# Dense FFN and output projections: 512 and 128 tokens in place of twice 320 per weight block

## The reference, cut to what matters

```python
def trunk_layer(x, cond, l, p, ctx, rope):
    ...
    mix, new_ctx = token_mixer(modulate(x, p['norm_mix'][l], sh_m, sc_m), p, l, ctx, rope)   # ends in mixed @ w_out[l]
    x = x + g_m * mix
    h = modulate(x, p['norm_ffn'][l], sh_f, sc_f)
    f = swiglu(h, ffn_w_gu, ffn_w_down)          # layer 0
    return x + g_f * f

def swiglu(h, w_gu, w_down):
    g, u = jnp.split(h @ w_gu, 2, axis=-1)
    return (jax.nn.silu(g) * u) @ w_down
```

## Time and profile before

| | |
|---|---|
| median of 3 runs | 2766.9 us (2763.91 to 2770.16) |
| profiled execution, its own time | 2763.11 us |
| its span, first to last instruction | 2761.4 us |
| TensorE matmuls / weight loads busy | 2425.1 us / 2202.9 us |
| VectorE, ScalarE busy | 1454.2 us, 1068.7 us |
| TensorE's mean granted clock | 0.93 |

### The profile page before, as it was taken

One profiled execution on the slowest core, in us unless ns is written; L12 is line 12 of the kernel. 1 busy time (PEld: TensorE's weight loads), 2 busy tenths in 40 slices (PEclk: granted clock), 3 DMA queues, 4 the chain that ended last, 5 costly groups with the idle time before them and its releaser, 6 DMA issues. The chain is left out here.

```text
span 2761.4 us, 47069 instructions
## 1 busy us (share of the span) xinstructions
PE 2425.1 (88%) x19300; PEld 2202.9 (80%) x19300; DVE 1454.2 (53%) x2061; ACT 1068.7 (39%) x1753; POOL 319.4 (12%) x340
## 2 busy tenths in 40 slices
PE   6995778988899999989967788886999999999993
PEld 4984555777899999989845657786899999999992
DVE  5576555675422222245765646753455555455556
ACT  4332235673422122142321456733444444354443
POOL 0055333000000000000642320002000000000002
PEclk8998897998999999999978969997999999999996
DMA  5333756502222322223136200024775676567654
GB/s 211 88 83 61 217 178 203 192 1 78 61 77 58 86 76 65 60 55 94 46 75 199 73 1 1 1 61 146 214 213 177 195 234 201 172 213 228 197 176 166
DMA packets 453116, 340.49 MB, mean 123 GB/s; under 512 B 90961, under 2 KB 421151, under 8 KB 451935
## 3 DMA queue, kind: packets, MB, share of 16 engines
q1 hardware_dynamic: 436383, 277.43, 34.6%
q10 hardware_dynamic: 11520, 41.95, 4.7%
q0 software_dynamic: 5056, 18.88, 1.8%
HBM read 287.68 MB, written 50.53 MB: 122 GB/s over the span
## 5 line engine op out<-in xcount | busy, mean ns | idle before, releaser
L2294 PE MATMUL ps<-h_hi,w_hi 128*128 128x256 f32 x1408 | 398.9, 283 | 2.1 <-DVE h_lo L2437 2.1
L2294 PE MATMUL ps<-h_hi,w_lo 128*128 128x256 f32 x1408 | 398.6, 283 | 0.0
L2294 PE MATMUL ps<-h_lo,w_hi 128*128 128x256 f32 x1408 | 398.5, 283 | 0.0
L2445 DVE TENSOR_TENSOR w_lo<-w_raw,w_hi 128x2048 fp32r<-128x2048 f32 (+1 forms) x180 | 309.1, 1756 | 118.9 <-ACT w_hi L2343 118.9
L2294 PEld LDWEIGHTS ps<-h_hi,w_hi 128*128 128x128 f32 x1408 | 270.0, 192 | 5.1 <-issue 2.3
L2294 PEld LDWEIGHTS ps<-h_lo,w_hi 128*128 128x128 f32 x1408 | 270.0, 192 | 2.8
L2294 PEld LDWEIGHTS ps<-h_hi,w_lo 128*128 128x128 f32 x1408 | 270.0, 192 | 0.0
L2343 ACT CAST w_hi<-w_raw 128x2048 fp32r<-128x2048 f32 (+1 forms) x180 | 256.4, 1473 | 0.1
L2678 PE MATMUL ps<-ffn_h_hi,w_hi_ffn 128*128 128x320 f32 x704 | 161.5, 311 | 5.5 <-DVE ffn_h_lo L378 4.2
L2678 PE MATMUL ps<-ffn_h_lo,w_hi_ffn 128*128 128x320 f32 x704 | 161.2, 310 | 0.0
L2678 PE MATMUL ps<-ffn_h_hi,w_lo_ffn 128*128 128x320 f32 x704 | 161.0, 310 | 0.0
(11 more groups left out here) (442 smaller groups left out, 5619.8 us busy)
## 6 DMA issues: line engine op xcount, KB each, us to landing
w_raw<-in_moe_w_gu SPq DMA_DIRECT2D x182, 512.0 KB, 5.1
w_raw<-in_moe_w_down SPq DMA_DIRECT2D x91, 512.0 KB, 5.9
G_decay<-in_ada_w ACTq DMA_DIRECT2D x54, 512.0 KB, 5.0
w_ahead<-in_ffn_w_gu SPq DMA_DIRECT2D x44, 512.0 KB, 5.2
slots_h<-tm SPq DMA_DIRECT2D x13, 1024.0 KB, 11.1
slots_y<-tm SPq DMA_DIRECT2D x12, 1024.0 KB, 11.2
w_ahead<-in_ffn_w_down SPq DMA_DIRECT2D x16, 704.0 KB, 4.7
oA<-in_ada_w ACTq DMA_DIRECT2D x20, 512.0 KB, 5.0
```

Source lines behind the costliest of these rows:

```text
L2294: mm = pe.matmul(ps[:, j % 2, half * BLK:(half + 1) * BLK], gu(wt, j, half, k), x[:, k, :], start=(k == 0 and n == 0), stop=(k == KC - 1 a ...
L2445: dve.tensor_tensor(wlo[:, q, part], raw[:, q, part], whi[:, q, part].bitcast(F32), ALU.subtract).then_inc(s["lo_d" if down else "lo_u"], 1)
```

## The change

A new constant WIDE, ((0, 512), (512, 640)), takes the place of HALVES, ((0, 320), (320, 640)), in the output projections and the dense FFN: the matmuls of each weight block now move 512 tokens and then 128, into the same two banks. ScalarE's Silu and VectorE's product go by the same pieces. In PIECES the cut between the banks moves too, so that `add_chunk` takes 0 to 128, 128 to 512 and 512 to 640. The norms and the input projection keep HALVES.

```diff
-PIECES = ((0, P, 0, 0), (P, T // 2, 0, 1), (T // 2, T, 1, 1))
+WIDE = ((0, 512), (512, T))
+PIECES = ((0, P, 0, 0), (P, 512, 0, 1), (512, T, 1, 1))
...
                             for n, (wt, x) in enumerate(((ws.hi, self.mhi), (ws.hi, self.mlo), (ws.lo, self.mhi))):
-                                for j, (a, b) in enumerate(HALVES):
+                                for j, (a, b) in enumerate(WIDE):
                                     mm = pe.matmul(ps[:, 2 * (m % 4) + j, 0:b - a], wt[:, m % 2, k * P:(k + 1) * P], x[:, k, a:b],
...
         for a, b, half, j in PIECES:
             x = self.xT[:, m, a:b]
-            a0 = HALVES[half][0]
+            a0 = WIDE[half][0]
...
                                     for m, (wt, x) in enumerate(((ws.hi, hhi), (ws.hi, hlo), (ws.lo, hhi))):
-                                        for st, (a, b) in enumerate(HALVES):
+                                        for st, (a, b) in enumerate(WIDE):
                                             mm = pe.matmul(ps[:, 4 * (j % 2) + 2 * half + st, 0:b - a], wt[:, u, o:o + P], x[:, k, a:b],
...
                                 for m, (wt, x) in enumerate(((ws.hi, ahi), (ws.hi, alo), (ws.lo, ahi))):
-                                    for st, (a, b) in enumerate(HALVES):
+                                    for st, (a, b) in enumerate(WIDE):
                                         mm = pe.matmul(ps[:, 2 * (m_ % 4) + st, 0:b - a], wt[:, u, j * P:(j + 1) * P], x[:, j, a:b],
...
-                            for st, (a, b) in enumerate(HALVES):
+                            for st, (a, b) in enumerate(WIDE):
                                 act.activation(sg[:, n % 2, a:b], ps[:, 4 * (n % 2) + st, 0:b - a], ACT.Silu).then_inc(s["silu"], 1)
...
-                            for st, (a, b) in enumerate(HALVES):
+                            for st, (a, b) in enumerate(WIDE):
                                 dve.wait_ge(s["silu"], 2 * c + st + 1)
                                 g = sg[:, n % 2, a:b]
                                 dve.tensor_tensor(g, g, ps[:, 4 * (n % 2) + 2 + st, 0:b - a], ALU.mult).then_inc(s["prod"], 1)
```

## The result

The changed kernel takes 2865.47 us (median of 4 runs, 2860.34 to 2869.57) against 2766.66 for the one before (4 runs): a ratio of 1.0362, 95% interval 1.035 to 1.0375. It is slower by 98.8 us; forecast were 91.6 us and 2858 us, with a range of 2838 to 2902. The profiled execution took 2860.3 us, with a span of 2858.6.

The account below looks back on a forecast made before the run. TensorE's matmul stream was taken to bound the kernel. Pairs 89.7, half clock 1.6 and bare chain 0.3 sum to 91.6 us, giving 2854.7 us on the profiled execution and 2858 on the median; range 2838 to 2902.

Parts of the forecast that it names:

- The load of the wide matmul: Edited matmul lines: its weight load has only the 128-wide matmul as cover, so pairs grow 45.6 ns, 89.7 us in all.
- The size, 112 ns for that step: Edited lines: a 128-wide matmul lasts as long as the next weight load, 112 ns, with bounds 104 to 122.
- The one-column rows: Trace of the kernel before: ten one-column matmuls whose weight loads come 115 and 111 ns apart, taken as the load's length.
- Half clock: First 6 to 10 us of matmul bursts: the half-speed loss grows with a pair's period, +1.6 us if it doubles.
- the bare chain: Where down matmuls wait for the last tile's Silu and product: unequal pieces add 0.15 us net, twice, 0.3 us.
- Rival A: Edited lines: the narrow matmul is cover enough for the load, a pair stays 293.1 ns, 2767 us; chance 0.07.
- The straight line through 320 and 512 columns: Matmul time from two measured widths: 0.418 ns a column plus 12.9 ns fixed, so 66.4 ns for 128 columns.
- formula for the gap: The Trainium skill's rule for back-to-back matmuls: columns / 2.4 plus 2.5 ns, a pair 271.7 ns before and after.
- Rival B: Edited lines: recorded narrow-matmul starts at face value, a 55 ns step, a pair 281.7 ns, gain 22 us, 2745 us; chance 0.03.
- the 12.9 ns fixed: Part of each matmul's time independent of its columns, from the 320- and 512-wide steps.
- Rival C: Edited lines: the whole 134 ns between loads is the price, 67.6 ns a pair, 133 us, 2902 us; chance 0.10.
- The signs given: Profile after: starts in turns of 0.23 and 0.11 us, pair 0.339, FFN 551 us, projections 67, longer ScalarE and VectorE waits.

Follow-up runs that it names:

- experiment 1: Changed kernel with 512-wide matmuls taking only 64 of 128 weight columns, 128-wide ones all: down pair 286.8 ns, total 2758.05 us.
- experiment 2: Changed kernel with 128-wide matmuls taking only 64 of 128 weight columns, 512-wide ones all: pairs 340.0 to 343.4 ns, total 2866.57 us.
- 3: Changed kernel with 512-wide matmuls taking 96 of 128 weight columns: down pair 313.4 ns, total 2822.16 us.
- 4: Changed kernel with the cut at 448 (448 and 192 tokens), all computed: 2813.22 us, +44.6 on the kernel before.
- experiment 5: Changed kernel with the cut at 384 (384 and 256 tokens), all computed: 2765.95 us against 2765.47 for the kernel before, ratio 1.0006.
- 9: Changed kernel with the 128-token piece of each weight block before the 512-token one, all computed: 2852.57 us beside 2762.5 for the kernel before.
- experiment 6: Changed kernel with the 512-wide matmuls left out of the three edited lines: 213 ns a step at granted clock 0.50, total 2608.9 us.
- experiment 11: Changed kernel run once more unaltered: 2871.49 us; up bursts 346.7 and 343.3 ns a pair, down bursts 340.0.
- experiment 10: Kernel cut at 448 with its 448-wide matmuls left out of the edited lines: 111 ns a step, granted clock 0.91, total 2449.34 us.
- experiment 8: Changed kernel with, from the second up tile on, all gate-block matmuls before all up-block ones: up line 345.0 ns a pair, total 2872.74 us.

## Why the prediction was right

**The load of the wide matmul is what the change uncovers: right, and shown.** Experiments 1 and 2 shorten one load each (and with it the output features of that matmul), with the same moving columns, 3 gives the slope, 4 and 5 the point where it begins (192 columns too few, 256 enough), 9 that identical weights don't help. The Trainium skill (TensorE: Matmul & The Clock Gate, section LDWEIGHTS) has a load as columns / 1.2 per ns: the measured 0.83 ns a column of the down line agrees, with 6.7 ns on top, but only at the full clock; at half clock the load took 213 ns (experiment 6).

**The size, 112 ns for that step: 113.3 in the down line and projections, 116.6 to 120 in the up line.** The one-column rows gave the value almost exactly. The forecast had 45.6 ns a pair and 89.7 us for all. Measured over the full-clock pairs it is 345.0 - 293.3 = 51.7 ns x 1056 = 54.6 us for the up line, 46.7 x 528 = 24.7 for the down line and 46.7 x 384 = 17.9 for the projections, 97.2 us. Of the 7.5 us missing, 1968 x 1.1 = 2.2 come from the load (113.3 in place of 112, less the 0.2 by which 293.1 was low), and 1056 x 5.0 = 5.3 are the up line's slower rhythm, for which the trace of before gave no sign: with 320 columns both lines had 293.3 a pair.

**Half clock and the bare chain, 1.6 and 0.3 us: their sum is near, in part by luck.** The stretches grew by 99.9 us, 2.7 more than the pairs account for. TensorE's wait for the last tile's chain grew from 6.3 to 6.6 us; by the forecast's own 1 ns a column its sum is 2 x 0.19, not 2 x 0.15, which is as near. The half clock at the start of the bursts cost 2.0 us more than before (each burst's length less its steps at full clock). But 1.2 of these 2.0 lie in the first down burst alone, whose first 6 us had a granted clock of 0.51 where they had 0.72 before. In the second profile of the same kernel (experiment 11) they had 0.72 again, so this part is not the loss that the forecast let grow with the period of a pair:

```profile
932.00:938.00 6.00, 5.79 (x25) 5.03 (x26) 1.69 (x2) 0.47 (x1) 0.00 (x0) 0.72 0.40 117
```

(The 0.69 from 738 to 748 against 0.74 in the earlier trace rows says little: that stretch begins 1.1 us before its burst's first matmul, the one of before 0.6 us.) Another 0.9 us has no term in the forecast at all. Between the last matmul of the first projection and the first of the FFN, ten of the loads for the one-column sums ran at half clock, 2.21 us where the earlier trace rows have 1.19:

```profile
727.30 2.21 PEld L2071 LDWEIGHTS ps<-cst,x_sq 128*128 128x128 f32 x10 [1.02 <-ACT x_sq L2055]
```

That is some 0.21 us from load to load, the step of experiment 6 in the changed kernel itself.

**Rival A, cover is enough (2767 us): wrong.** The straight line through 320 and 512 columns holds down to 256 (experiment 5), and the load takes over below. The Trainium skill's formula for the gap (same page, section Back-to-back issue gap) fails with it; the page itself says that the formula is for a matmul alone and has no budget for the load, which the prediction did not mention.

**Rival B, starts at face value (2745 us): wrong, with a grain of truth.** The 57 to 61 ns between the recorded starts are there after the change as well, at 340 ns a pair: the recorded start is no sign that the matmul runs. But a 128-wide matmul can be as short as 60 ns where the load allows it (experiment 1), so the 12.9 ns fixed are not a constant for narrow ones.

**Rival C, 134 ns (2902 us): wrong.** The 0.13 us between two loads in the earlier trace rows held more than the load, as supposed. No run says what.

**The signs given** came out but for one: pairs of about 0.34 us, 512-wide matmuls recorded longer, ScalarE and VectorE waiting longer. The FFN's stretch is 558.9 us, not 551; a projection has 67. The granted clock over the FFN is unchanged. Wrong was that the matmuls' starts would come in turns of 0.23 and 0.11 us: they come in turns of 0.28 and 0.06 (970.04 to 970.32 to 970.38 in the down tile). It is the loads that come 0.11 and 0.23 apart (970.32, 970.43, 970.66). Whoever looks for the wait in the matmuls' starts alone would take the narrow matmul for quick and the wide one for slow.

## What to carry to other kernels

Of a matmul and the weight load that runs beside it, the longer one counts: with float32r and 128 weight columns here the load needs 113 ns, which a matmul of 256 moving columns covered and one of 192 did not. Split a moving dimension so that every piece covers the load, evenly or not; of the four cuts measured here a full bank and a narrow rest was the worst (512 and 128: +98.8 us; 448 and 192: +44.6; 384 and 256: no difference from twice 320). Look for the load's length in a place of the trace where matmuls have almost no columns, not in the matmuls' busy share, which doesn't show this wait at all.

## What was not expected of the hardware

A stream of 128-wide float32r matmuls with full loads, back to back for 352 us, ran at a granted clock of 0.50 throughout (experiment 6), while the same stream with 192 columns had 0.91 (experiment 10). The one with half loads, in which TensorE also waited for other engines, rose and fell between both levels (0.80 over the stage). TensorE had been busy for 340 of the 352 us in the profile and did not rise; why stays open. A study that isolates narrow matmuls can so measure the lower level without meaning to. In the changed kernel's FFN this did not matter (0.99).

The exposed pair has rhythms 3.3 ns apart, 340.0, 343.3 and 346.7 ns, and a burst of 528 or 1056 matmuls keeps one from its second tile on. Which one differed between two profiles of the same kernel (experiment 11). In the changed kernel the up line had the two upper ones and the down line the lowest each time; in experiment 2 the first down burst had 340.0 and the second 346.7, so it isn't bound to the line. What sets it stays open; the order of the blocks is not it (experiment 8).
